# Tokens and the first two weight blocks in four parts on two queues, multiplied step by step together

## The reference, cut to what matters

```python
proj = x @ w_in[l]                      # x: 256 x 1024, w_in: 1024 x 6144
conv_u = proj[..., :Q_OFF]              # 2048 columns: a, gate of the conv branch
q, k, v = ...                           # attention
gates = jax.nn.sigmoid(proj[..., G_OFF:] + b_gate[l])
a, gate = jnp.split(conv_u, 2, axis=-1)
h = a * jax.nn.sigmoid(gate)            # then a depthwise conv of width 31 over tokens
...
moe = hierarchical_moe(x, ...)          # 32 experts, 3 MB of weights each
```

## Time and profile before

| | |
|---|---|
| time, median of 3 runs | 495.59 us (495.35 to 497.16) |
| the profiled execution: its own time | 495.22 us |
| its span | 493.0 us |
| TensorE busy | 470.1 us (95% of the span) |
| VectorE, ScalarE, GpSimd busy | 245.6, 202.4, 223.2 us |
| chain that ended last: TensorE's share | 86% |

### The profile page before, as it was taken

How to read it: one execution, slowest core, us unless ns; L and a number is a source line. 1 busy time by engine, 2 the same in 40 slices (tenths; PEclk the granted TensorE clock), 3 DMA queues, 4 the chain that set the end, 5 groups by cost and what they waited for, 6 DMA issues and landing times.

```text
span 493.0 us, 7686 instructions
## 1 busy us (share of the span) xinstructions
PE 470.1 (95%) x2816; PEld 333.0 (68%) x2816; DVE 245.6 (50%) x536; ACT 202.4 (41%) x447; POOL 223.2 (45%) x187
## 2 busy tenths in 40 slices
PE   7999999999999999999998999999999999889992
PEld 6999999898999999988973544444444434334431
DVE  1089999759996445640689242222222222122116
ACT  3544554498875696554542242221221211122112
POOL 3899899766865778999308021111111110011002
PEclk9999999999999999999998999999999999989997
DMA  8799988523533445549938999999999999999702
GB/s 289 255 362 367 362 296 329 196 104 120 181 128 129 130 170 169 175 172 364 423 150 320 361 368 427 422 418 423 420 421 421 423 419 421 422 420 422 292 0 86
DMA packets 26370, 145.13 MB, mean 294 GB/s; under 512 B 3040, under 2 KB 3296, under 8 KB 13792
## 3 DMA queue, kind: packets, MB, share of 16 engines
q1 hardware_dynamic: 26336, 144.67, 74.7%
HBM read 143.61 MB, written 1.05 MB: 293 GB/s over the span
## 4 chain that ended last, share of the span: by engine, by line
PE 86%; DVE 5%; ACT 3%; issue 2%; DMA 2%; SPq 1%; POOL 1%; DVEq 0%; ACTq 0%
PE bank L1493 21%; PE bank L1245 12%; PE bank L1528 12%; PE bank L1247 12%; PE bank L1246 12%; PE bank L1543 3%; PE bank L1544 3%; DMA raw<-in_w_in 2%; PE bank L1323 1%; PE bank L1301 1%; PE bank L1517 1%; DVE info L1132 1%; POOL w_lo L497 1%; PE bank L1467 1%; PE bank L1468 1%
## 5 line engine op out<-in xcount | busy, mean ns | idle before, releaser
L497 POOL TENSOR_TENSOR w_lo<-raw,w_hi 128x512 fp32r<-128x512 f32 x140 | 183.1, 1326 | 46.9 <-ACT w_hi L562 43.6
L562 ACT CAST w_hi<-raw 128x512 fp32r<-128x512 f32 x140 | 85.2, 620 | 80.5 <-PE bank L1247 75.6
L1245 PE MATMUL bank<-x_hi,w_hi 128*128 128x256 f32 x400 | 115.5, 289 | 1.4 <-POOL w_lo L497 1.4
L1247 PE MATMUL bank<-x_hi,w_lo 128*128 128x256 f32 x400 | 113.2, 283 | 0.0
L1246 PE MATMUL bank<-x_lo,w_hi 128*128 128x256 f32 x400 | 113.1, 283 | 0.0
L523 POOL COPY raw<-gates 128x512 f32 x28 | 19.8, 706 | 161.0 <-PE bank L1493 140.9
L808 DVE SCALAR_TENSOR_TENSOR bank<-slots,par,bank 128x256 f32<-128x256 f32 x232 | 92.3, 481 | 0.2
L1493 PE MATMUL bank<-slots,raw 128*64 128x512 f32 x320 | 84.5, 592 | 0.0
L1245 PEld LDWEIGHTS bank<-x_hi,w_hi 128*128 128x128 f32 x400 | 76.6, 192 | 2.1 <-issue 1.3
L1246 PEld LDWEIGHTS bank<-x_lo,w_hi 128*128 128x128 f32 x400 | 76.7, 192 | 0.3
L1247 PEld LDWEIGHTS bank<-x_hi,w_lo 128*128 128x128 f32 x400 | 76.7, 192 | 0.0
(11 more groups left out here) (213 smaller groups left out, 655.8 us busy)
## 6 DMA issues: line engine op xcount, KB each, us to landing
slots<-in_w_gate_up SPq DMA_DIRECT2D x40, 1024.0 KB, 13.5
slots<-in_w_down SPq DMA_DIRECT2D x32, 1024.0 KB, 15.9
raw<-in_w_in SPq DMA_DIRECT2D x48, 512.0 KB, 4.2
extra<-in_w_gate_up SPq DMA_DIRECT2D x8, 1024.0 KB, 12.0
spare<-in_w_gate_up SPq DMA_DIRECT2D x8, 1024.0 KB, 16.0
late<-in_w_gate_up SPq DMA_DIRECT2D x8, 1024.0 KB, 18.7
raw<-in_w_attn SPq DMA_DIRECT2D x8, 512.0 KB, 3.3
raw<-in_w_conv SPq DMA_DIRECT2D x8, 512.0 KB, 3.3
```

The lines of the kernel that those rows point to most:

```text
L497: nc.gpsimd.tensor_tensor(w_lo[:, n % SPLIT, m], raw[:, b % RAW, m], w_hi[:, n % SPLIT, m].bitcast(F32), ALU.subtract).then_inc(w_lo_done, 1)
L562: nc.scalar.copy(w_hi[:, n % SPLIT, m], raw[:, b % RAW, m]).then_inc(w_hi_done, 1)
L1245: mm(dst, ah, bh, start=first, stop=False, **kw)
L1247: return mm(dst, al, bh, start=False, stop=last, **kw)
```

## The change

Tokens are loaded in four parts (two slices `k` each, 256 KB) on SP's queue. The two native blocks are loaded in four parts each (128 KB) by ScalarE, on its own queue; one semaphore `first_loaded[g]` counts the three loads of part `g`. TensorE takes the 16 native matmuls in the order of `k`, both blocks at each `k`. The token split goes in four parts. Constants: `par` is loaded behind block 3, the other three behind block 5; VectorE waits for them at blocks 5 and 24. There is one warm-up matmul fewer. Since the native blocks' parts no longer count on `raw_loaded`, ScalarE's wait count is adapted.

```diff
-WARM_START, WARM_NORM, WARM_TURN, WARM_ROUTE, WARM_PLACE = 3, 2, 1, 11, 2
+WARM_START, WARM_NORM, WARM_TURN, WARM_ROUTE, WARM_PLACE = 2, 2, 1, 11, 2
+FIRST_PARTS = 4
+PART_K = KT // FIRST_PARTS
@@ sync
-            for c in range(2):
-                sp.dma_start(xT_raw[:, 4 * c:4 * c + 4, :], xT[:, 4 * c:4 * c + 4, :]).then_inc(s_xT[c], 16)
-                sp.dma_start(raw[:, c, :], block_of(c)).then_inc(raw_loaded[c], 16)
+            for g in range(FIRST_PARTS):
+                n = slice(g * PART_K, (g + 1) * PART_K)
+                sp.dma_start(xT_raw[:, n, :], xT[:, n, :]).then_inc(first_loaded[g], 16)
...
-                if b == 2:
+                if b == 3:
                     sp.dma_start(par[:], chan).then_inc(s_par, 16)
+                if b == 5:
                     sp.dma_start(con[:], consts).then_inc(s_con, 16)
                     sp.dma_start(dist, dists).then_inc(s_dist, 16)
                     sp.dma_start(row[:], rows.broadcast_to([P, R_END])).then_inc(s_row, 16)
@@ scalar
-            for c in range(2):
-                act.wait_ge(s_xT[c], 16)
-                nc.scalar.copy(x_hi[:, 4 * c:4 * c + 4, :], xT_raw[:, 4 * c:4 * c + 4, :]).then_inc(x_hi_done, 1)
+            for g in range(FIRST_PARTS):
+                for b in NATIVE:
+                    m = slice(g * PART_K * P, (g + 1) * PART_K * P)
+                    act.dma_start(raw[:, b, m], block_of(b)[:, m]).then_inc(first_loaded[g], 16)
+            for g in range(FIRST_PARTS):
+                n = slice(g * PART_K, (g + 1) * PART_K)
+                act.wait_ge(first_loaded[g], 16 * (1 + len(NATIVE)))
+                nc.scalar.copy(x_hi[:, n, :], xT_raw[:, n, :]).then_inc(x_hi_done, 1)
@@ vector (the token split goes in four parts too)
                 if b == 2:
                     dve.wait_ge(consts_set, 4)
+                if b == 5:
                     dve.wait_ge(s_par, 16)
+                if b == 24:
                     dve.wait_ge(s_con, 16)
                     dve.wait_ge(s_row, 16)
                     dve.wait_ge(s_dist, 16)
@@ tensor
+            def native_blocks():
+
+                for k in range(KT):
+                    if k % PART_K == 0:
+                        pe.wait_ge(first_loaded[k // PART_K], 16 * (1 + len(NATIVE)))
+                    for b in NATIVE:
+                        ins = mm(pair_bank[0][:, b * SEQ:(b + 1) * SEQ], raw[:, b, k * P:(k + 1) * P], xT_raw[:, k, :],
+                                 start=(k == 0 and b == 0), stop=(k == KT - 1), skip_group_check=True)
+                        if k == KT - 1:
+                            ins.then_inc(block_done, 1)
...
-            for b in range(N_IN):
+            native_blocks()
+            for b in range(len(NATIVE), N_IN):
```

More of the change, by code:

```diff
@@ L72, with loads_of_raw @@
 NATIVE = (0, 1)
+FIRST_PARTS = 4
+PART_K = KT // FIRST_PARTS
 def split_block(n):
     return [b for b in range(N_BLOCKS) if b not in NATIVE][n]
+def loads_of_raw(b):
+    return b // RAW + 1 - (b % RAW in NATIVE)
 def splits_before(b):
@@ L275, in encoder_kernel @@
         gu_bank, y_bank, turn_bank = bank[0], [bank[1], bank[2]], bank[7]
-        s_xT = [sem(f"s_xT{c}") for c in range(2)]
+        first_loaded = [sem(f"first_loaded{g}") for g in range(FIRST_PARTS)]
         s_con, s_par, s_row, s_xt = (sem(n) for n in ("s_con", "s_par", "s_row", "s_xt"))
@@ L553, in split_hi @@
             def split_hi(b):
-                act.wait_ge(raw_loaded[b % RAW], 16 * (b // RAW + 1))
+                act.wait_ge(raw_loaded[b % RAW], 16 * loads_of_raw(b))
                 n = splits_before(b)
@@ L581, in evacuate @@
                         act.wait_ge(s_par, 16)
-                        act.wait_ge(x_lo_done, 2)
+                        act.wait_ge(x_lo_done, FIRST_PARTS)
                     for j in range(2):
@@ L932, in split_o @@
                                         ALU.subtract).then_inc(o_lo_done, 1)
-            for c in range(2):
-                k = slice(4 * c, 4 * c + 4)
-                dve.wait_ge(x_hi_done, c + 1)
+            for g in range(FIRST_PARTS):
+                k = slice(g * PART_K, (g + 1) * PART_K)
+                dve.wait_ge(x_hi_done, g + 1)
                 nc.vector.tensor_tensor(x_lo[:, k, :], xT_raw[:, k, :], x_hi[:, k, :].bitcast(F32),
@@ L1255, in column_block @@
                 n = splits_before(b)
-                if b in NATIVE:
-                    pe.wait_ge(raw_loaded[b % RAW], 16 * (b // RAW + 1))
                 for k in range(KT):
-                    if b not in NATIVE and k % 4 == 0:
+                    if k % 4 == 0:
                         pe.wait_ge(w_lo_done, 2 * n + k // 4 + 1)
@@ L1263, in column_block @@
                     w = slice(k * P, (k + 1) * P)
-                    if b in NATIVE:
-                        if b == 0 and k % 4 == 0:
-                            pe.wait_ge(s_xT[k // 4], 16)
-                        ins = mm(dst, raw[:, b % RAW, w], xT_raw[:, k, :], start=(k == 0), stop=(k == KT - 1))
-                    else:
-                        ins = three_products(dst, ((w_hi[:, n % SPLIT, w], w_lo[:, n % SPLIT, w]),
-                                                   (hi[:, k, :], lo[:, k, :])), k == 0, k == KT - 1)
-                        if k == 3:
-                            ins.then_inc(half_done, 1)
-                ins.then_inc(block_done, 1)
+                    ins = three_products(dst, ((w_hi[:, n % SPLIT, w], w_lo[:, n % SPLIT, w]),
+                                               (hi[:, k, :], lo[:, k, :])), k == 0, k == KT - 1)
+                    if k == 3:
+                        ins.then_inc(half_done, 1)
+                ins.then_inc(block_done, 1)
+            def native_blocks():
[7 more added lines that the diff above has]
+                            ins.then_inc(block_done, 1)
             def value_block(b):
@@ L1342, in _ @@
                 mm(bank[3][:, c * SEQ:(c + 1) * SEQ], ones[:], warm, start=(c == 0), stop=True, skip_group_check=True)
-            for b in range(N_IN):
+            native_blocks()
+            for b in range(len(NATIVE), N_IN):
                 if b == 2:
-                    pe.wait_ge(x_lo_done, 2)
+                    pe.wait_ge(x_lo_done, FIRST_PARTS)
                 if b == 24:
```

## The result

| | before | changed |
|---|---|---|
| median, 11 runs each | 495.61 us (494.39 to 498.48) | 498.31 us (496.49 to 499.87) |
| ratio, 95% interval | | 1.0054 [1.0037, 1.0072] |
| profiled execution: own time, span | 495.22, 493.0 us | 498.74, 496.9 us |

Slower by 2.7 us (by the interval 1.8 to 3.6). The forecast was 494.5 us, and the top of its range 496.6.

A forecast was written before the change was run, and what follows sets the result against it. TensorE, with 86% of the chain of waits, was taken as the bound. 495.22 us less 0.7 (natives) and 0.4 (block 3's wait) gave 494.1, plus 0.37 to the median: 494.5 us, 8-in-10 range 493.0 to 496.6.

The forecast's parts named there:

- Near the lower bound: 5.5 us: Start of the natives: part 0's 512 KB would be there at 5.5 us, between bounds of 5.35 and 6.64.
- The 7% that I took for short rows: Early loads: rate loss from shorter rows, 0.4 us on 2 MB if it held for all; 0.2 us taken.
- If the parts come in order none after the first is waited for: Native matmuls: a part every 1.3 us against 1.8 us of work, so TensorE would be free at 12.3 us.
- The slower rival: Early loads: the second queue gets the smaller share, so weight parts come late; 496.0 us, or 496.4 against the median; chance 0.2.
- One warm-up matmul less: TensorE before the natives: shortens work that ended at 5.25 us by 0.4 us, inside idle time; counted as nothing.
- TensorE's pace: Native matmuls: less warm-up and stops between parts may slow them, up to +1.7 us, giving 495.8 us; chance 0.05.
- Cast at 10.48 as before: ScalarE's cast of block 2: same bytes ahead of it, so no sooner than 10.48 us, at best.
- No wait at block 3: Block 3 on TensorE: earlier load has its first half ready at 15.2, wanted at 15.8 us; 0.4 us gained.
- Hidden, by 1.5 us: Block 6's load behind the moved constants: lands near 21.0 us, wanted at 22.5, so no cost.
- Block 4's late load, the other rival: Block 4's load takes 5.0 us, TensorE waits 1.0 us: no change, 495.1 us or 495.5 against the median; chance 0.15.
- I take the whole gain through: From start to end of kernel: later loads follow TensorE's progress, so the whole 1.1 us gain reaches the end.
- 0.92 for less than 2.5 us either way: Whole kernel time: chance 0.92 of "same", within 2.5 us of 495.6, against 0.05 faster and 0.03 slower.

The follow-up runs named there:

- e13: Kernel before, but ScalarE issues the two native blocks' loads, each whole, while SP issues the tokens in two halves and then block 2; ratio 1.0028 [1.0007, 1.0050].
- e1: Changed kernel, but SP also issues the eight weight parts, each pair behind its token part, and ScalarE issues nothing; ratio 1.0001 [0.9977, 1.0026].
- e6: Changed kernel, but SP issues block 2 and all that follows only once part 1 has landed; ratio 1.0032 [1.0010, 1.0054].
- e7: Changed kernel with the queues swapped: SP loads the eight weight parts, ScalarE the four token parts; ratio 1.0048 [1.0021, 1.0076].
- e12: Kernel before, first half of tokens in two loads around block 0, constants moved back as far as `row` behind block 12; ratio 0.9991 [0.9970, 1.0013].
- e11: Changed kernel with two first parts instead of four, so longer rows and half the issues; ratio 1.0068 [1.0040, 1.0096].
- e9: e6 with the third warm-up matmul put back; ratio 1.0037 [1.0016, 1.0059].
- e10: Changed kernel with the third warm-up matmul put back, nothing else; ratio 1.0052 [1.0031, 1.0074].
- e2: Kernel before with only the constants moved: `par` behind block 3, the others behind block 5, VectorE's waits moved too; ratio 0.9993 [0.9970, 1.0016].
- e5: Kernel before with 12 more warm-up matmuls, so the natives start later; ratio 1.0080 [1.0052, 1.0107].
- e4: Changed kernel with all four constant loads put back behind block 2, ahead of block 3; ratio 1.0076 [1.0047, 1.0105].
- e8: Changed kernel, but `row` is read from 128 separate source rows instead of one row 128 times; one execution, 499.74 us.
- e3: Changed kernel with only the load of `row` moved, from behind block 5 to behind block 12; ratio 1.0061 [1.0040, 1.0082].
- e14: Kernel before with its first four loads each cut in two by partitions (64 each, 4 KB rows), on SP's one queue; ratio 1.0054 [1.0034, 1.0073].

## Why the prediction was wrong, step by step

**"Near the lower bound: 5.5 us"** failed: 6.80. I assumed that bytes arrive at the rate of before whatever their rows. In the first 5 us 0.82 MB (216 packets) moved before, 0.87 in e13 with whole rows on two queues, but 0.53, 0.47, 0.52 and 0.49 in the changed kernel, e1, e6 and e7, in 341 to 364 packets, 0.61 in e12, and 0.68 in e11 with rows of 4 and 2 KB. The same loads scatter: e9, whose loads up to there are e6's, moved 0.60. The row length and the size of a load go with it, not the second queue. Whether the price is one of each packet or of each small load is not separated, and so the cause of this step's failure stays open. The 7% that I took for short rows, from a full stretch, was the wrong row: of the 0.40 MB that are missing at 12 us, 0.29 are missing at 5 us.

**"If the parts come in order none after the first is waited for"** is the step that failed most. The parts did not come in order with SP's loads: parts 2 and 3 were cast at 13.23 and 14.16, and block 2 began at 16.80 instead of 12.75, where e9, without the overtaking and at full pace, has 14.86. The slower rival was right in kind, and e6 and e7 show it; it was priced too low (parts 2 and 3 at 11.2 and 12.3, block 3 at 17.8, 496.4 us), because it took the bytes of before: by 12 us 3.11 MB had moved (4 x 81, then 208, 362, 333, 324, 2 x 420 and 2 x 359 GB/s), not 3.51. SP's bytes were through but for 0.07 MB and ScalarE's were the last. The Trainium skill, "DMA: Bandwidth & Descriptors", section "Queues, rings and completion order", has an engine alternate between queues packet by packet. The traces agree: 950 and 1006 packets by 12 us for 2.19 and 0.92 MB with unequal rows, 117 and 94 packets for 0.48 and 0.39 MB by 5 us with equal ones (e13). What the trace counts as a packet is here about one row long (0.92 MB in 1006 packets of 1 KB rows); packets of several rows, of which the prediction speaks, are not seen in it. The Trainium skill, "DMA: Bandwidth & Descriptors", section "Issuing engines are not separate DMA queues", says that a second issuer saves only issue time. The start of e13 agrees (6.59 us against 6.64). I had priced the second queue at nothing, which left out that the queues now compete.

**Issues and pace.** ScalarE's eight issues ended at 5.51 us, where I had 3.9 to 5.2; the table load behind them made the first cast (6.84) no later than the part. *"One warm-up matmul less"*, priced at nothing, left 1.72 us without work ahead of the natives, and they ran 1.65 us slower (the rival "TensorE's pace", priced at up to 1.7): hidden in the changed kernel (e10), bare in e6 against e9.

**Block 2 and block 3.** "Cast at 10.48 as before" failed twice. Block 2 landed 8.6 us after its issue at 2.77, near 11.4. And it was cast only at 14.68, when block 3 had landed too: ScalarE casts `x_hi` part 3 first, which waits for the weights of the natives too. A wait in a stream in order holds back what stands behind it. "No wait at block 3" was right (e2 as well), 0.4 us that no median here can show.

**"Hidden, by 1.5 us" (constants behind block 5)** was wrong in the changed kernel's profiled execution: block 6's load went from issue at 18.87 to its cast at 28.03, 9.16 us, and TensorE lost 1.60. In e10 the same order took 7.39 us and was just covered, and in e2 it was. I had counted 680 KB at 400 GB/s and left out the dip that `row` brings, about 1.3 us for its 22 KB. Block 4's late load, the other rival, did not bite: loaded 3.1 us after issue (16.57 to 19.71), and TensorE had it at 22.62 without a wait, since block 3 was as late.

**"I take the whole gain through"** held for the sign: e5's 3.6 us came out as 3.8. Microsecond for microsecond the table doesn't show it (router 1.7 later and no loss in e1, 1.1 later and 0.37% in e9): one profiled execution stands there beside the median of many.

Right: the first rows' bytes gain nothing by a second issuer, block 3's wait, block 4. Wrong: the sign of the change, and 0.92 for less than 2.5 us either way, which 2.7 us just exceed (the interval reaches from 1.8 to 3.6), since the case with the real cause was priced 2 us short.

## What to carry to other kernels

Before splitting a load over a second queue, ask which loads already in the first may now overtake it: here the two queues shared by packets, and the one with the long rows took 2.19 of 3.11 MB. Cutting rows from 4 KB to 1 KB to start sooner can take away at the start what the smaller need gave; splitting for order only pays if the first part is there sooner, which is one row to check. A constant that is read many times from one source row asks for more slack behind it than its bytes say, here about 1.3 us for 22 KB. And before a wait in one profiled execution is given a cause, look for the same loads in another kernel's trace.

## What the runs showed of the hardware that I had not expected

- Two queues with rows of 1 KB and of 2 and 4 KB: 0.15 against 0.38 MB in 5 us, 0.92 against 2.19 in 12, at 1006 against 950 packets; with equal rows of 4 KB 0.39 against 0.48 MB in 5 us.
- Loads with rows of 1 and 2 KB among them moved 0.46 to 0.61 MB in the first 5 us (e4 and e12 are the ends), e11's of 2 and 4 KB 0.68, whole rows 0.82 to 0.87, at a like share of busy time (0.42 and 0.45 up to 4 us).
- Some 4 us after the issue of a load that reads one 176-byte source row 128 times the rate fell to 125 GB/s for 2 us (e10), where 374 flowed with 128 source rows (e8).
- Loads over 64 partitions ran at 225 to 246 GB/s with all engines' share at 1.0.
- After 1.59 to 1.76 us without work, behind four warm-up matmuls (the changed kernel, e3, e6, e8), TensorE's records took 0.43 instead of 0.22 us for 3 to 6 us; after 1.35 (e1) and 1.50 us (e7) behind four and 1.35 behind five (e9) 0.22 at once. After 2.28 us behind five (e14) it was slow again. The granted clock column read 1.00 in all of them. After 2.46 (e4) and 3.81 us (e11) behind four the pace was the same slow one and the column read 0.50.
